# Sample attention scores: the query at 8r of 32 columns, a column strip per chunk, and a new order around it

## The chip, the cores and the metric

One core of one Trainium2 chip runs the whole program. The metric is the device time of one execution in microseconds (us). TensorE is PE in the profile (its weight loads PEld), VectorE DVE, ScalarE ACT, GpSimd POOL, the DMA-issuing SyncE SP.

## The reference, cut to what matters

The program is one decoder layer: an input projection, latent attention and retention, their merge, a convolutional feed-forward. It works on a prompt of 512 + 16 tokens and on 8 samples of one token each, with a paged cache of 4096 positions per sample. The change touches only the latent attention of the samples:

```
q_abs = einsum('bthn,chn->bthc', q_nope, w_uk)                     # 8 heads, 256 latent dims
s_past = einsum('bthc,bsc->bhts', q_abs, c_past) + einsum('bthr,bsr->bhts', q_rope, kr_past)
s_new  = einsum('bthc,buc->bhtu', q_abs, c_new) + einsum('bthr,bur->bhtu', q_rope, kr_new)
p = softmax(concat([s_past, s_new]) * scale)
o_lat = einsum('bhts,bsc->bthc', p_past, c_past) + einsum('bhtu,buc->bthc', p_new, c_new)
```

c_past is 4096 x 256 and kr_past 4096 x 32 for each of the 8 samples. Everything is float32.

## The kernel before

Each engine has its own program; semaphores tie them. Prompt attention comes before the stage of interest, the merge and the feed-forward after it. The stage handles the 8 samples one after the other. A sample's pages are cut into 8 chunks of 512 positions. POOL gathers a chunk (512 KB) with one indirect DMA (`chunk`, line 569) into `pages_c`, which has two halves, one for even and one for odd samples; a gather overwrites what the sample two before had there. In POOL's loop (lines 595 to 604) the gather of chunk c waits until PE has weighed chunk c of that earlier sample (`pv_chunk`, line 1984); the rope rows and the indices of the sample wait for `s_full`, the earlier sample's finished scores.

On PE, one call of `sample` (line 1989) is one step. A step mixes two samples: it scores sample b, and for sample b - 1 does the softmax's small parts and the weighing. Its blocks:
- `turn_chunk` (line 1910): eight 128 x 128 transposes bring a chunk's latent dims onto the partitions, into PSUM banks 0, 1 (even chunks) or 2, 3 (odd). ACT (`even_back`) or DVE (`odd_back`) copies them to `pages_T`; the next turn into the same banks waits for that copy. `pages_T` holds four chunks, so a copy also waits until the chunk four before has been scored.
- `score_pair` (line 1922): two chunks at once. The stationary operand is the query, 32 columns of which 8 (the heads) are filled; the four pages r of a chunk go to the four strips of 32 columns, 256 moving columns each. ACT copies the results (`parts_back`) and `add_parts` turns them with small matmuls onto bank 6, on which `score_rope` has put the rope part (one matmul a chunk, 128 stationary and 32 moving columns).
- `score_new` adds the sample's own token; DVE then takes the scores and their maxima (`scores_back`).
- `max_turn`, `max_spread`, `sum_spread`: the maximum over partitions and the sum, each a small PE operation between two DVE operations; `exp_sample` on ACT lies between them.
- `weigh_chunk` (line 1974): probabilities times pages, four matmuls a chunk in the four strips. The first waits for the exponentials and for the reciprocal of the sum (`inv_sum`).
- `latent_turn`: the weighted sum back onto partitions, after DVE's copy (`outputs_back`).

The order on each engine is written out by hand in `sample` (PE), `sample_dve` (DVE) and `sample_act` (ACT). PE weighs chunks 0 and 1 of sample b - 1 after the second score pair, 2 to 4 after the third, then turns chunks 0 and 1 of sample b + 1 (whose gathers went into the half just weighed), and weighs 5 to 7 after the fourth pair. Steps 1 to 6 gather again in this way; the pages of samples 0 and 1 are gathered ahead of the stage.

Of the kernel before, what the change touches and what calls it, by code (L numbers as in the profile page):

```python
# [146 lines left out]
def build(nc, ins, outs):  # L147
    ctx = ExitStack()
    with ctx:
# [53 lines left out]
        def plan(start, *items):  # L203
# [34 lines left out]
        (PGR, SCB, PB, QRB, SSM, OL, SPART, OPART, QNW, QRW), e4 = plan(  # L238
# [40 lines left out]
        def score_width(t):  # L279
# [20 lines left out]
                 "rope_back chunk_turned odd_turned ct_act ct_dve pair_scored q_staged parts_back "  # L300
# [314 lines left out]
        def _(act):  # L615
# [211 lines left out]
            ct, scored, shifted = Count(S["chunk_turned"]), Count(S["pair_scored"]), Count(S["shifted"])  # L827
            rope_t = Count(S["rope_turned"])

            def even_back(c, reuse=0):  # L830
                act.wait_ge(ct.sem, ct.after())
                if reuse:
                    act.wait_ge(scored.sem, scored.after(reuse))
                nc.scalar.activation(CT[:, c % 4].rearrange("p a b -> p (a b)"),
                                     PS[:, 0:2, :].rearrange("p a b -> p (a b)"), ACT.Copy
                                     ).then_inc(S["ct_act"], 1)
# [5 lines left out]
            def parts_back(a):  # L842
                act.wait_ge(scored.sem, scored.after())
                nc.scalar.activation(SPART[:, a, :], PS[:, 4 + a, :], ACT.Copy).then_inc(S["parts_back"], 1)
# [30 lines left out]
            sample_act(1, True, False)  # L875
            exp_sample(1)
# [122 lines left out]
        def _(dve):  # L999
# [311 lines left out]
            V.memset(PB[:, :, 33:36, :], 0.0).then_inc(S["olat_ready"], 1)  # L1311
# [3 lines left out]
            ct_o, s_full, scored = Count(S["odd_turned"]), Count(S["s_full"]), Count(S["pair_scored"])  # L1315
# [4 lines left out]
            def stage_query(par, b):  # L1320
                V.tensor_copy(QNW[:, par, :, 0:HEADS], QAB[:, :, bass.ds(b, 1), :].rearrange("p a b h -> p a (b h)"))
# [3 lines left out]
            def odd_back(c, reuse=True):  # L1325
                dve.wait_ge(ct_o.sem, ct_o.after())
                if reuse:
                    dve.wait_ge(scored.sem, scored.after())
                V.tensor_copy(CT[:, c % 4].rearrange("p a b -> p (a b)"),  # L1329
# [46 lines left out]
            def sample_dve(par, b, prev=True, more=True, first=False):  # L1376

                if prev:
                    max_rows(1 - par)
                odd_back(3, not first)  # L1380
                if prev:
                    shift(1 - par)
                    sum_rows(1 - par)
                odd_back(5)
                if prev:
                    inv_sum(1 - par)
                if more:
                    stage_query(1 - par, b + 1)
                odd_back(7)
                if more:  # L1390
                    odd_back(1)
                if prev:
                    outputs_back()
                scores_back(par, b)
                if prev:
                    latent_out(1 - par, b - 1)

            stage_query(0, 0)
            odd_back(1, False)
            sample_dve(0, 0, prev=False, first=True)  # L1400
            with loop(dve, 3, {chain: 4, ct_o: 8, scored: 8, mxt: 2, mxs: 2, exp_s: 2, sums: 2, s_full: 2,
                               bank_free: 2, pv_full: 2, lat_turned: 2}) as i:
                for par in range(2):
                    sample_dve(1 - par, i * 2 + (1 + par))
            sample_dve(1, DEC - 1, more=False)
            max_rows(1)
# [165 lines left out]
        def _(pe):  # L1572
# [349 lines left out]
            def score_pair(par, p):  # L1922


                two_chunks = slice(2 * (p % 2), 2 * (p % 2) + 2)
                for ct in range(2):
                    for r in range(4):
                        last = T.matmul(PS[32 * r:32 * r + 32, 4 + p // 2, 256 * (p % 2):256 * (p % 2) + 256  # L1928
                                           ].rearrange("p (a b) -> p a b", a=2),
                                        QNW[:, par, ct, :], CT[:, two_chunks, ct, P * r:P * (r + 1)],  # L1930
                                        start=ct == 0, stop=ct == 1, skip_group_check=True)
                last.then_inc(S["pair_scored"], 1)

            def score_rope(par, c):
# [270 lines left out]
```

## Time and profile before

| | us |
|---|---|
| median of 3 runs (lowest, highest) | 1296.41 (1295.78, 1297.62) |
| profiled execution, its own time | 1295.44 |
| its span, first to last instruction | 1293.6 |
| PE busy | 1151.9 (89%) |
| DVE, ACT, POOL busy | 562.7, 399.2, 109.0 |
| mean granted PE clock | 0.935 |

A clock of 1.00 is 2.4 GHz, 0.50 is 1.2 GHz. In rows in order of time, the first number is the start from the span's begin, the second the duration of the merged instructions, xN their count; an idle time of the engine ahead of them and its releaser stand in brackets. An f32 matmul appears as two instructions, a transpose as one.

### The profile page before, as it was taken

The numbers are of one execution on the slowest core, as the hardware profiler recorded it, in microseconds if no ns is written. First come the engines' busy times: TensorE is split into PE (matmuls) and PEld (weight loads), VectorE is DVE, ScalarE is ACT, GpSimd is POOL, SyncE is SP. The second block draws the span as 40 slices with busy tenths as digits, with TensorE's granted clock in tenths as the row PEclk, the third lists the DMA queues.
The fourth block names the chain that finished last, engine by engine and source line by source line (L and its number), as shares of the span: only waits on it lengthen the run. The fifth ranks groups of instructions, "written<-read, shape, count | busy, mean of one in ns | idle before, by whom it ended". The sixth has DMA issues, their size and how long they took to land.

```text
span 1293.6 us, 22217 instructions
## 1 busy us (share of the span) xinstructions
PE 1151.9 (89%) x9006; PEld 1044.0 (81%) x9006; DVE 562.7 (44%) x901; ACT 399.2 (31%) x645; POOL 109.0 (8%) x99
## 2 busy tenths in 40 slices
PE   2899988879999997999996889679999999999991
PEld 1899887767878786777774889679999999999991
DVE  7256643363534444343342451644444213444226
ACT  3222321213232423323331122344553123443112
POOL 3000002000000002243420000210000000000003
PEclk9989997879999998999996899769999999999995
DMA  9312347113314002475642564113322253232201
GB/s 271 98 52 66 83 99 234 48 33 89 84 31 115 33 33 85 145 243 195 225 166 83 153 174 121 33 34 97 85 77 73 73 146 99 80 83 61 82 21 69
DMA packets 168466, 131.67 MB, mean 102 GB/s; under 512 B 19052, under 2 KB 151489, under 8 KB 168401
## 3 DMA queue, kind: packets, MB, share of 16 engines
q1 hardware_dynamic: 155880, 88.95, 24.8%
q0 software_dynamic: 10368, 37.75, 8.5%
q10 hardware_dynamic: 2176, 4.39, 0.9%
q8 instruction: 29, 0.48, 0.2%
q14 instruction: 13, 0.10, 0.0%
HBM read 119.27 MB, written 11.90 MB: 101 GB/s over the span
## 4 chain that ended last, share of the span: by engine, by line
PE 82%; DVE 11%; ACT 2%; issue 2%; DMA 1%; POOL 0%; SPq 0%; POOLq 0%; ACTq 0%; DVEq 0%; PEldq 0%
PE PS L1584 47%; PE PS L1790 8%; PE PS L1918 5%; PE PS L1595 3%; PE PS L1981 3%; PE PS L1928 2%; PE PS L1828 2%; DVE stats L1028 1%; PE PS L1935 1%; PE PS L1817 1%; DVE y_tok L1033 1%; DVE x_tok L1033 1%; PE PS L1942 1%; PE PS L1805 1%; DVE w_lo L1010 1%
## 5 line engine op out<-in xcount | busy, mean ns | idle before, releaser
L1584 PE MATMUL PS<-x_hi,w_hi 128*128 128x268 f32 x1056 | 226.6, 297 | 8.0 <-DVE w_lo L1010 4.0
L1584 PE MATMUL PS<-x_lo,w_hi 128*128 128x268 f32 x1056 | 222.0, 292 | 0.0
L1584 PE MATMUL PS<-x_hi,w_lo 128*128 128x268 f32 x1056 | 221.1, 292 | 0.0
L1010 DVE TENSOR_TENSOR w_lo<-w_raw,w_hi 128x2048 fp32r<-128x2048 f32 (+3 forms) x65 | 130.6, 2009 | 160.8 <-ACT w_hi L628 160.5
L1584 PEld LDWEIGHTS PS<-x_hi,w_hi 128*128 128x128 f32 x1056 | 171.4, 196 | 12.9 <-DVE w_lo L1010 4.4
L1584 PEld LDWEIGHTS PS<-x_lo,w_hi 128*128 128x128 f32 x1056 | 171.3, 195 | 0.0
L1584 PEld LDWEIGHTS PS<-x_hi,w_lo 128*128 128x128 f32 x1056 | 169.8, 194 | 0.0
L628 ACT ACTIVATE w_hi<-w_raw 128x2048 fp32r<-128x2048 f32 (+3 forms) x65 | 109.5, 1684 | 119.5 <-PE PS L1584 75.1
L1790 PE MATMUL PS<-x_hi,w_hi 128*128 128x268 f32 x256 | 79.7, 311 | 0.0
L1584 PE MATMUL PS<-ffn_hi,w_hi 128*128 128x268 f32 x352 | 73.8, 292 | 5.2 <-DVE ffn_lo L1525 5.2
L1790 PE MATMUL PS<-x_hi,w_lo 128*128 128x268 f32 x256 | 74.3, 290 | 0.0
L1790 PE MATMUL PS<-x_lo,w_hi 128*128 128x268 f32 x256 | 74.2, 290 | 0.0
L549 POOL TENSOR_TENSOR y_tok<-y_tok,ln_gb 128x1024 f32<-128x1024 f32 (+1 forms) x10 | 23.4, 2343 | 596.6 <-ACT y_tok L641 596.6
L1584 PE MATMUL PS<-ffn_hi,w_lo 128*128 128x268 f32 x352 | 73.4, 290 | 0.0
L1584 PE MATMUL PS<-ffn_lo,w_hi 128*128 128x268 f32 x352 | 73.1, 289 | 0.0
L1918 PE MATMUL PS<-square_consts,pages_c 128*128 128x128 f32 x512 | 64.1, 279 | 6.9 <-DVE q_now L1312 6.3
L569 POOL DMA_INDIRECT pages_c<-in_cache_kv_latent_dram,page_rows_now x64 | 61.9, 968 | 82.2 <-PE PS L1981 67.9
L1329 DVE COPY pages_T<-PS 128x1024 f32<-128x1024 f32 x32 | 39.2, 1224 | 66.6 <-PE PS L1918 62.5
L1918 PEld LDWEIGHTS PS<-square_consts,pages_c 128*128 128x128 f32 x512 | 57.2, 144 | 13.4 <-issue 13.1
L1584 PEld LDWEIGHTS PS<-ffn_hi,w_hi 128*128 128x128 f32 x352 | 56.2, 193 | 5.7 <-issue 5.7
L1584 PEld LDWEIGHTS PS<-ffn_lo,w_hi 128*128 128x128 f32 x352 | 56.1, 192 | 0.0
L1584 PEld LDWEIGHTS PS<-ffn_hi,w_lo 128*128 128x128 f32 x352 | 56.0, 192 | 0.0
(291 smaller groups left out, 1847.3 us busy)
## 6 DMA issues: line engine op xcount, KB each, us to landing
w_raw<-in_w_ffn_in_dram SPq DMA_DIRECT2D x44, 512.0 KB, 5.0
w_raw<-in_w_in_dram SPq DMA_DIRECT2D x37, 512.0 KB, 6.2
w_raw<-in_w_ffn_out_dram SPq DMA_DIRECT2D x16, 384.0 KB, 3.9
w_raw<-in_w_ffn_out_dram SPq DMA_DIRECT2D x16, 320.0 KB, 3.5
gate_scratch<-gate_out ACTq DMA_DIRECT2D x8, 536.0 KB, 2.9
gates<-gate_scratch SPq DMA_DIRECT2D x8, 536.0 KB, 4.9
w_raw<-in_w_o_dram SPq DMA_DIRECT2D x8, 512.0 KB, 5.1
x_tok<-in_x_prompt_dram SPq DMA_DIRECT2D x4, 512.0 KB, 8.0
```

Source lines behind the costliest of these rows:

```text
L569: nc.gpsimd.indirect_dma_start(out=PGC[:, par, 4 * c:4 * c + 4, :].rearrange("p r c -> p (r c)"), out_offset=None, in_=lat_rows, in_offset ...
L628: nc.scalar.activation(WH[:, par, 0:nk], RAW[:, par, 0:nk], ACT.Copy).then_inc(s_whi, 1)
L1010: V.tensor_tensor(WL[:, par, 0:nk], RAW[:, par, 0:nk], WH[:, par, 0:nk].bitcast(F32), ALU.subtract).then_inc(s_wsplit, 1)
L1033: V.scalar_tensor_tensor(x[0:r, t, :], x[0:r, t, :], MV[0:r, t, 0:1], gain[0:r, 0, :], ALU.subtract, ALU.mult).then_inc(chain.sem, 1)
L1329: V.tensor_copy(CT[:, c % 4].rearrange("p a b -> p (a b)"), PS[:, 2:4, :].rearrange("p a b -> p (a b)")).then_inc(S["ct_dve"], 1)
L1584: last = T.matmul(PS[:, bank, 0:HALF], w[:, par, k, m * P:(m + 1) * P], x[:, k0 + k, half * HALF:(half + 1) * HALF], start=start and k == ...
L1595: last = T.matmul(PS[:, 2 * p + half, 0:HALF], a, b[:, half * HALF:(half + 1) * HALF], start=i == 0, stop=i == len(lhs) - 1)
L1790: last = T.matmul(PS[:, half, 0:HALF], w[:, par, k, m * P:(m + 1) * P], x[:, k, half * HALF:(half + 1) * HALF], start=k == 0 and w is WH a ...
L1828: last = T.matmul(out, VB[0:w, k, rows_], PTS[0:w, hh, k, 0:r], start=k == 0, stop=k == t)
L1918: last = T.transpose(PS[:, 2 * (c % 2) + ct, P * r:P * (r + 1)], PGC[:, par, 4 * c + r, ct * P:(ct + 1) * P], IDENT)
L1928: last = T.matmul(PS[32 * r:32 * r + 32, 4 + p // 2, 256 * (p % 2):256 * (p % 2) + 256].rearrange("p (a b) -> p a b", a=2), QNW[:, par, ct ...
L1981: last = T.matmul(PS[32 * r:32 * r + 32, 7, 256:256 + KVL], PB[:, par, k:k + 4, :].rearrange("p k h -> p (k h)"), PGC[:, par, k, :], start ...
```

## The change

- The staged query has four copies, copy r with the 8 heads at columns 8r of 32. `score_half` scores four chunks (a = 0 for chunks 0 to 3, a = 1 for 4 to 7) at once: chunk g goes to column strip g, page r accumulates through copy r of the query, so that one strip's 32 rows are 4 pages x 8 heads and a matmul has 128 moving columns. It is called in two halves, pages 0 and 1, then 2 and 3; the second half also adds the rope part, one matmul a chunk, into the same strips.
- The results of four chunks are one 128 x 128 tile; `turn_parts` turns it with one transpose.
- `pages_T` holds eight chunks, so fewer copies wait for scores; `rope_T` moves elsewhere, `score_parts` shrinks to 128 columns.
- The order in `sample`, `sample_dve` and `sample_act` is new: the second half of a sample's second group of scores, its parts, `score_new` and `scores_back` lie in the next step, and `latent_turn` lies in the step after the weighing. Chunks 0 to 3 are weighed in one block just ahead of the turn of the next sample's chunk 0, and 4 to 7 in another. What was left over from step 7 follows it. POOL's program is not changed.

```diff
-        (PGR, SCB, PB, QRB, SSM, OL, SPART, OPART, QNW, QRW), e4 = plan(
+        (PGR, SCB, PB, QRB, SSM, OL, SPART, OPART, QNW, QRW, RTT), e4 = plan(
             65536, ("pages_r", [P, 2, NPAGES, ROPE]), 
...
-            ("score_parts", [P, 2, 512]), ("out_parts", [P, KVL]), ("q_now", [P, 2, 2, 32]), ("q_rope_now", [P, 2, 32]))
-
-        CT = nc.alloc_sbuf_tensor_at("pages_T", [P, 4, 2, 512], F32, offset=base)
-        RTT = nc.alloc_sbuf_tensor_at("rope_T", [P, 2, NCH, P], F32, offset=base + 4 * 2 * 512 * 4)
-        assert (4 * 2 * 512 + 2 * NCH * P) * 4 <= 2 * KT * COLS * 4
+            ("score_parts", [P, 2, P]), ("out_parts", [P, KVL]), ("q_now", [P, 2, 2, 4, 32]), ("q_rope_now", [P, 2, 32]),
+            ("rope_T", [P, 2, NCH, P]))
+
+        CT = nc.alloc_sbuf_tensor_at("pages_T", [P, NCH, 2, 512], F32, offset=base)
+        assert NCH * 2 * 512 * 4 <= 2 * KT * COLS * 4
 
...
 
                 even_back(2)
                 if prev:
+                    parts_back(1)
+                even_back(4)
+                if prev:
                     exp_sample(1 - par)
-                even_back(4, 1)
+                even_back(6)
                 parts_back(0)
-                even_back(6)
                 if more:
+                    even_back(0)
                     rope_back(1 - par, 0, 4)
-                    even_back(0, 1)
-                else:
-                    scored.add()
-                parts_back(1)
-                if more:
                     rope_back(1 - par, 1, 4)
 
...
+                    V.tensor_copy(QNW[:, par, :, r, HEADS * r:HEADS * (r + 1)],
+                                  QAB[:, :, bass.ds(b, 1), :].rearrange("p a b h -> p a (b h)"))
                 V.tensor_copy(QRW[:, par, :], QRB[:, bass.ds(b, 1), :, :].rearrange("p b g h -> p (b g h)")
                               ).then_inc(S["q_staged"], 1)
 
-            def odd_back(c, reuse=True):
+            def odd_back(c, wait=1):
...
                 V.tensor_copy(OPART[:], PS[:, 7, 256:256 + KVL]).then_inc(S["o_parts"], 1)
 
-            def sample_dve(par, b, prev=True, more=True, first=False):
-
+            def sample_dve(par, b, prev=True, more=True, older=True):
+
+                if prev and older:
+                    outputs_back()
+                odd_back(3, 0)
+                if prev:
+                    if older:
+                        latent_out(par, b - 2)
+                    scores_back(1 - par, b - 1)
+                odd_back(5, 2 if prev else 0)
                 if prev:
                     max_rows(1 - par)
-                odd_back(3, not first)
+                    shift(1 - par)
+                odd_back(7, 0)
                 if prev:
-                    shift(1 - par)
                     sum_rows(1 - par)
-                odd_back(5)
-                if prev:
                     inv_sum(1 - par)
                 if more:
                     stage_query(1 - par, b + 1)
-                odd_back(7)
-                if more:
-                    odd_back(1)
-                if prev:
-                    outputs_back()
-                scores_back(par, b)
-                if prev:
...
-                T.matmul(PS[:, 6, 32 * c:32 * c + 32], RTT[:, par, c, :], QRW[:, par, :], start=c == 0, stop=False,
-                         skip_group_check=True)
-
-            def add_parts(a):
+            def score_half(par, a, half):
+
+
+                for r in range(2 * half, 2 * half + 2):
+                    for ct in range(2):
+                        for g in range(4):
+                            last = T.matmul(PS[32 * g:32 * g + 32, 4 + a, 0:P], QNW[:, par, ct, r, :],
+                                            CT[:, 4 * a + g, ct, P * r:P * (r + 1)], start=r == 0 and ct == 0, stop=False,
+                                            skip_group_check=True)
+                if half:
+                    for g in range(4):
+                        last = T.matmul(PS[32 * g:32 * g + 32, 4 + a, 0:P], QRW[:, par, :], RTT[:, par, 4 * a + g, :],
+                                        start=False, stop=True, skip_group_check=True)
+                last.then_inc(S["half_scored"], 1)
+
+            def turn_parts(a):
 
                 pe.wait_ge(parts.sem, parts.after())
-                for c in range(4):
-                    T.matmul(PS[:, 6, 32 * (4 * a + c):32 * (4 * a + c) + 32], SPART[:, a, P * c:P * (c + 1)],
-                             SMALL[:, 26:58], start=False, stop=a == 1 and c == 3, skip_group_check=True)
+                T.transpose(PS[:, 6, P * a:P * (a + 1)], SPART[:, a, :], IDENT)
 
             def score_new(par):
                 out = PS[0:DEC, 6, 256:264]
                 for ct in range(2):
-                    T.matmul(out, CN8[:, ct, :], QNW[:, par, ct, 0:HEADS], start=False, stop=False, skip_group_check=True)
...
                     T.matmul(PS[0:HEADS, 7, 256:256 + KVL], PB[0:DEC, par, 32, :], CTX[0:DEC, :], start=False, stop=True,
                              skip_group_check=True).then_inc(S["pv_full"], 1)
 
-            def sample(par, prev=True, more=True):
+            def sample(par, prev=True, more=True, older=True):
 
 
                 turn_chunk(par, 2)
+                if prev and older:
+                    latent_turn()
                 turn_chunk(par, 3)
                 if prev:
-                    pe.wait_ge(olat.sem, olat.after())
-                    max_turn(1 - par)
+                    score_half(1 - par, 1, 1)
+
+                turn_chunk(par, 4)
+                if prev:
+                    turn_parts(1)
+                    score_new(1 - par)
+                turn_chunk(par, 5)
                 pe.wait_ge(q_staged.sem, q_staged.after())
                 pe.wait_ge(rope_back.sem, rope_back.after(1 if prev else 2))
-                score_pair(par, 0)
+                score_half(par, 0, 0)
+                if prev:
+                    if older:
+                        pe.wait_ge(olat.sem, olat.after())
+                    max_turn(1 - par)
+
+                turn_chunk(par, 6)
                 if prev:
                     max_spread(1 - par)
-
-                turn_chunk(par, 4)
-                turn_chunk(par, 5)
-                score_pair(par, 1)
+                turn_chunk(par, 7)
+                score_half(par, 0, 1)
                 if prev:
                     sum_spread(1 - par)
-                    pe.wait_ge(bank_free.sem, bank_free.after())
-                for c in range(4):
-                    score_rope(par, c)
-                if prev:
-                    for c in range(2):
-                        weigh_chunk(1 - par, c)
-
-                turn_chunk(par, 6)
-                turn_chunk(par, 7)
-                score_pair(par, 2)
-                for c in range(4, 6):
-                    score_rope(par, c)
-                add_parts(0)
-                if more:
-                    turn_rope(1 - par, 0, 4)
-                if prev:
-                    for c in range(2, 5):
+                    for c in range(4):
                         weigh_chunk(1 - par, c)
 
                 if more:
                     turn_chunk(1 - par, 0)
+                    if prev:
+                        pe.wait_ge(bank_free.sem, bank_free.after())
+                    turn_parts(0)
                     turn_chunk(1 - par, 1)
+                    turn_rope(1 - par, 0, 4)
                 else:
+                    pe.wait_ge(bank_free.sem, bank_free.after())
+                    turn_parts(0)
                     pe.wait_ge(ct_a.sem, ct_a.after())
                     pe.wait_ge(ct_d.sem, ct_d.after())
-                score_pair(par, 3)
-                for c in range(6, NCH):
-                    score_rope(par, c)
+                score_half(par, 1, 0)
                 if prev:
-                    for c in range(5, NCH):
+                    for c in range(4, NCH):
                         weigh_chunk(1 - par, c)
                 if more:
                     pe.wait_ge(rope_back.sem, rope_back.after())
                     turn_rope(1 - par, 1, 4)
-                add_parts(1)
-                score_new(par)
-                if prev:
-                    latent_turn()
 
             rope_back, q_staged, parts = Count(S["rope_back"]), Count(S["q_staged"]), Count(S["parts_back"])
...
```

On ACT `parts_back` now waits for two `half_scored` and copies 128 columns; the loops on PE and DVE run twice two steps, with steps 0, 1, 6 and 7 written out.

## Rows read from the trace of the kernel before

**Rows 1.** The page: busy time, share and instructions; the chain by engine.
```profile
PE 1151.9 (89%) x9006; PEld 1044.0 (81%) x9006; DVE 562.7 (44%) x901; ACT 399.2 (31%) x645; POOL 109.0 (8%) x99
...
PE 82%; DVE 11%; ACT 2%; issue 2%; DMA 1%; POOL 0%; SPq 0%; POOLq 0%; ACTq 0%; DVEq 0%; PEldq 0%
```

**Rows 2.** One step; busy time (x instructions) by engine, PE clock, DMA share, GB/s.
```profile
555.45:577.64 22.19, 22.19 (x251) 16.27 (x251) 8.53 (x19) 6.80 (x9) 8.65 (x11) 1.00 0.63 209
```

**Rows 3.** The same step, PE in order of time: start, duration, instruction, count.
```profile
557.43 1.07 PE L1928 MATMUL PS<-pages_T,q_now 128*32 128x256 f32 x16
558.43 0.38 PE L1958 MATMUL PS<-sm,square_consts 8*128 8x8 f32 x2
558.74 1.97 PE L1918 MATMUL PS<-square_consts,pages_c 128*128 128x128 f32 x16
560.64 1.07 PE L1928 MATMUL PS<-pages_T,q_now 128*32 128x256 f32 x16
561.64 0.39 PE L1963 MATMUL PS<-sm,square_consts 128*128 128x8 f32 x2
561.88 1.06 PE L1935 MATMUL PS<-q_rope_now,rope_T 128*128 128x32 f32 x8
562.87 1.07 PE L1981 MATMUL PS<-pages_c,p_sample 128*32 128x256 f32 x16
563.87 1.97 PE L1918 MATMUL PS<-square_consts,pages_c 128*128 128x128 f32 x16
...
567.24 1.06 PE L1942 MATMUL PS<-small_consts,score_parts 128*128 128x32 f32 x8
568.13 0.63 PE L1905 MATMUL PS<-square_consts,pages_r 128*128 128x128 f32 x4
568.70 1.50 PE L1981 MATMUL PS<-pages_c,p_sample 128*32 128x256 f32 x24
570.13 1.97 PE L1918 MATMUL PS<-square_consts,pages_c 128*128 128x128 f32 x16
...
577.64 1.95 PE L1918 MATMUL PS<-square_consts,pages_c 128*128 128x128 f32 x16
```

**Rows 4.** POOL in order of time: the gather of chunk 0.
```profile
564.35 0.94 POOL L569 DMA_INDIRECT pages_c<-in_cache_kv_latent_dram,page_rows_now  x1 [6.07 <-PE PS L1981]
```

**Rows 5.** Gathers' line 569, issue to landing: those issued at 564.35, 565.59, 571.42.
```profile
DMA to landing us min/median/max: 4.3/4.3/4.3
...
DMA to landing us min/median/max: 5.1/5.1/5.1
...
DMA to landing us min/median/max: 5.8/5.8/5.8
```

**Rows 6.** DVE and PE in order of time: one copy, then the tail.
```profile
565.88 1.23 DVE L1329 COPY pages_T<-PS 128x1024 f32<-128x1024 f32 x1 [3.11 <-PE PS L1918]
...
686.83 0.37 PE L1954 MATMUL PS<-square_consts,sm 128*8 128x128 f32 x1 [0.85 <-DVE o_lat L1367]
...
689.37 0.62 DVE L1356 TENSOR_REDUCE sm<-p_sample 128x8 f32<-128x264 f32 x1 [0.49 <-ACT p_sample L840]
...
690.05 0.60 PE L1963 MATMUL PS<-sm,square_consts 128*128 128x8 f32 x2 [1.63 <-DVE sm L1356]
691.04 6.37 PE L1981 MATMUL PS<-pages_c,p_sample 128*32 128x256 f32 x64 [0.39 <-DVE sm L1361]
```

**Rows 7.** Windows as in rows 2 at three places, and PE's first instruction after a pause.
```profile
512.40:515.60 3.20, 3.20 (x17) 3.20 (x16) 0.00 (x0) 1.85 (x3) 2.46 (x3) 0.50 0.94 321
515.80:519.20 3.40, 2.87 (x30) 2.36 (x32) 1.53 (x2) 1.09 (x2) 2.49 (x4) 1.00 0.98 361
...
737.60:744.30 6.70, 6.15 (x27) 6.16 (x28) 5.63 (x7) 1.80 (x2) 0.00 (x0) 0.50 0.02 2
...
738.15 0.81 PE L1584 MATMUL PS<-attn_hi,w_hi 128*128 128x268 f32 x2 [3.63 <-DVE w_lo L1010]
```

More of the change, by code:

```diff
@@ L842, in parts_back @@
             def parts_back(a):
-                act.wait_ge(scored.sem, scored.after())
-                nc.scalar.activation(SPART[:, a, :], PS[:, 4 + a, :], ACT.Copy).then_inc(S["parts_back"], 1)
+                act.wait_ge(scored.sem, scored.after(2))
+                nc.scalar.activation(SPART[:, a, :], PS[:, 4 + a, 0:P], ACT.Copy).then_inc(S["parts_back"], 1)
             def rope_back(par, half, bank):
@@ L1320, in stage_query @@
             def stage_query(par, b):
-                V.tensor_copy(QNW[:, par, :, 0:HEADS], QAB[:, :, bass.ds(b, 1), :].rearrange("p a b h -> p a (b h)"))
+                for r in range(4):
+                    V.tensor_copy(QNW[:, par, :, r, HEADS * r:HEADS * (r + 1)],
+                                  QAB[:, :, bass.ds(b, 1), :].rearrange("p a b h -> p a (b h)"))
                 V.tensor_copy(QRW[:, par, :], QRB[:, bass.ds(b, 1), :, :].rearrange("p b g h -> p (b g h)")
                               ).then_inc(S["q_staged"], 1)
-            def odd_back(c, reuse=True):
+            def odd_back(c, wait=1):
                 dve.wait_ge(ct_o.sem, ct_o.after())
-                if reuse:
-                    dve.wait_ge(scored.sem, scored.after())
-                V.tensor_copy(CT[:, c % 4].rearrange("p a b -> p (a b)"),
+                if wait:
+                    dve.wait_ge(scored.sem, scored.after(wait))
+                V.tensor_copy(CT[:, c].rearrange("p a b -> p (a b)"),
                               PS[:, 2:4, :].rearrange("p a b -> p (a b)")).then_inc(S["ct_dve"], 1)
@@ L1388, in sample_dve @@
                     stage_query(1 - par, b + 1)
-                odd_back(7)
-                if more:
-                    odd_back(1)
-                if prev:
-                    outputs_back()
-                scores_back(par, b)
-                if prev:
-                    latent_out(1 - par, b - 1)
+                    odd_back(1, 2)
             stage_query(0, 0)
-            odd_back(1, False)
-            sample_dve(0, 0, prev=False, first=True)
-            with loop(dve, 3, {chain: 4, ct_o: 8, scored: 8, mxt: 2, mxs: 2, exp_s: 2, sums: 2, s_full: 2,
+            odd_back(1, 0)
+            sample_dve(0, 0, prev=False)
+            sample_dve(1, 1, older=False)
+            with loop(dve, 2, {chain: 4, ct_o: 8, scored: 8, mxt: 2, mxs: 2, exp_s: 2, sums: 2, s_full: 2,
                                bank_free: 2, pv_full: 2, lat_turned: 2}) as i:
                 for par in range(2):
-                    sample_dve(1 - par, i * 2 + (1 + par))
+                    sample_dve(par, i * 2 + (2 + par))
+            sample_dve(0, DEC - 2)
             sample_dve(1, DEC - 1, more=False)
+            outputs_back()
+            latent_out(0, DEC - 2)
+            scores_back(1, DEC - 1)
             max_rows(1)
@@ L1947, in score_new @@
                 for ct in range(2):
-                    T.matmul(out, CN8[:, ct, :], QNW[:, par, ct, 0:HEADS], start=False, stop=False, skip_group_check=True)
+                    T.matmul(out, CN8[:, ct, :], QNW[:, par, ct, 0, 0:HEADS], start=ct == 0, stop=False,
+                             skip_group_check=True)
                 T.matmul(out, KR8[:], QRW[:, par, 0:HEADS], start=False, stop=True, skip_group_check=True
@@ L2053, in _ @@
             sample(0, prev=False)
+            sample(1, older=False)
             per = {ct_a: 8, ct_d: 8, bank_free: 2, mx: 2, dg: 2, sums: 2, rs: 2, olat: 2,
@@ L2056, in _ @@
             per.update({pages[j][c]: 1 for j in range(2) for c in range(NCH)})
-            with loop(pe, 3, per):
+            with loop(pe, 2, per):
                 for par in range(2):
-                    sample(1 - par)
+                    sample(par)
+            sample(0)
             sample(1, more=False)
+            latent_turn()
+            score_half(1, 1, 1)
+            turn_parts(1)
+            score_new(1)
             pe.wait_ge(olat.sem, olat.after())
```

25 lines of the change are left out of this document (7 added, 18 removed).

## The prediction

> **What bounds the kernel now.** I read four views in this order. The page first: PE is busy 89% of the span and 82% of the chain of waits is PE's, so a microsecond matters where PE runs without a gap [rows 1]. Then the busy time of one stage: in the sample scores, steps of 22.19 us (577.64 - 555.45), PE is busy all 22.19 us at granted clock 1.00 (2.4 GHz), DVE 8.5, ACT 6.8, POOL 8.6 [rows 2]. So PE's own instructions set the step; what other engines wait for costs nothing yet. Then PE in order of time, for the price of each block as the distance to the next block's start [rows 3]. Last the loop through PE, POOL and the gathers, which has no idle in it on PE today but little slack either [rows 3 to 5].
>
> **Prices of the blocks** [rows 3]. Two chunk turns (16 transposes) and the change to the scoring form: 560.64 - 558.74 = 1.90 us; a transpose alone is 0.109 (1.90 less 0.16 for the change of form, over 16), a chunk 0.87. A score_pair: 558.43 - 557.43 = 1.00 for 16 halves (every f32 matmul is issued as two). They run as four groups, one half in each 32-column strip at once: 1.00 = 4 x 0.215 + 0.14 for leaving the form. 256 columns in two passes at 2.4 GHz are 0.213, so the stream sets these 0.215. Rope matmuls: 8 halves 562.87 - 561.88 = 0.99. add_parts: 568.13 - 567.24 = 0.89 for 8 halves. Both load 128 columns for 32 that stream: 0.111 each. Weighing: 563.87 - 562.87 = 1.00 for two chunks, 570.13 - 568.70 = 1.43 for three, so 1.86 for four.
>
> **The matmuls.** Per sample the change takes out four pairs (4.00), eight rope matmuls (16 halves, about 2.02 with their changes of form) and eight part matmuls (1.80). It adds 64 score matmuls of 128 columns and 8 rope matmuls in the same strips: 144 halves, 36 groups of four. No row before has 32 stationary columns and 128 moving. Bounds of a group: the stream, half of 0.215 = 0.107; and 0.215, should a group of any width take what today's takes. I take 0.108: a transpose loads 128 columns and streams 128 in 0.109, so load and stream overlap fully there, and four strips of 32 columns load as much [rows 3]. 36 x 0.108 + 4 x 0.14 for the forms = 4.45. Two transposes of the parts add 0.22. Further the weighing goes in two blocks of four instead of 2, 3, 3 chunks: -0.14. Sum: 22.19 - 7.82 + 4.45 + 0.22 - 0.14 = 18.9; laying the after order out block by block gives 18.66, which I use: 3.5 us less PE work a step.
>
> The Trainium skill (TensorE: Matmul & The Clock Gate, section "Wait — 56ns, not 53.3ns?") gives a floor of about 62 ns per matmul where instructions go through the sequencer's code. A group of four would take 0.248 by it, whatever its width. The trace has such a group in 0.215 and single halves of rope at 0.111, so it does not bear the 62 ns out at once; the 0.215 end is rival two below.
>
> **What the new order uncovers.** I lay out step b from the start S of the turn of chunk 2.
> (a) S + 0 turn 2, latent_turn (four halves at 0.111 = 0.45), turn 3, second half of the last sample's second scores (1.22), turn 4, parts, new; turn 5 at S + 4.8; first half scores; maximum; turn 6; spread (0.31, [rows 3]); turn 7 at S + 8.2.
> (b) sum_rows now stands behind the copy of chunk 7 on DVE. Such a copy starts 1.14 after its turn (565.88 against 563.87 + 0.87) and takes 1.23, of which the next instruction overlaps a little: 1.16; PE's sum_spread starts 0.68 after the sum's start (690.05 - 689.37) [rows 3, 6]. So sum_spread is at turn 7 + 2.98, where PE alone would have it at + 2.26: a wait of 0.72.
> (c) Weighing waits for the reciprocal, and the four score_rope (0.99) that lay between are gone. sum_spread's two halves take 0.39, and at the tail, where nothing lies between either, PE idled 0.39 more for the reciprocal [rows 3, 6]: 0.78 where it is 0.24 today (561.88 - 561.64), a wait of 0.54. Weighing starts at W = S + 11.9. PE alone with (b) and (c) would need 19.9 a step.
> (d) The large one. Both samples' pages lie in two buffers. Chunk 0 of the next sample goes where chunk 0 of the last one is just being weighed, and POOL's gather waits for that. Today weighing starts at 562.87, POOL issues at 564.35 (+1.48) and the gather lands 4.3 later, at +5.8; PE wants it at 570.13, +7.3. The second chunk lands at 565.59 + 5.1 = +7.8, wanted at +8.1 [rows 3 to 5]. It is just in time. After the change turn 0 stands directly behind four weighed chunks: it wants chunk 0 at W + 1.86. The gather is unchanged: PE waits to W + 5.9, 4.0 us. Then the parts' transpose and turn 1, ready at W + 6.9, wants a gather that lands at W + 7.9: 1.0 more.
> (e) Rope turn and changes of form (568.70 - 568.13 = 0.57), scores (0.86), then weighing 4 to 7 at V. A burst's second gather takes 5.8 [rows 5]: chunk 5 lands at V + 2.72 + 5.8 = V + 8.5. The next S is at V + 2.9, its turn 5 at V + 7.7: a wait of 0.1 (landing 5.1) to 0.9; I take 0.5. In this part DVE, ACT and POOL (8.6 us of issue a step) are ahead of PE.
> (f) The clock. PE idles some 3.6 us in (d). After 3.63 us idle it was granted 0.50 (1.2 GHz) in 737.60 to 744.30 [rows 7]. At half clock turn 0 (0.87 more) hides in the wait for chunk 1, turn 1 and rope do not. From 0.7 us, if the clock is back after turn 1, to 2.2 us, if it covers rope and scores too; I take 1.1.
> Here the Trainium skill (TensorE: Matmul & The Clock Gate, Part 4: PE-mode transpose) says that transposes don't count as busy for the clock. Then it would stay low through turn 0, turn 1 and rope, and (f) would be 2.2 a step. The trace speaks against it: in 512.40 to 515.60 PE does transposes alone at 0.50, and in 515.80 to 519.20, begun with transposes, the clock is 1.00 [rows 7].
>
> A step: 19.9 + 4.0 + 1.0 + 0.5 + 1.1 = 26.5 against 22.2: +4.3.
>
> **The ends.** Step 0 weighs nothing and its next pages landed long before: it gains the matmul saving, and a half scoring of 1.2 us moves into step 1 instead; against it stand larger memset and staging copies ahead of the first turn (0.3) and a wait of 0.5 for the copy of chunk 3 on DVE. -3.7. Steps 1 to 6 gather again: 6 x 4.3 = 25.8, less 0.9 in step 1, which has no latent_turn and no late chunk 5: +24.9. Step 7 turns no next sample, so no (d); but latent_turn, half the second scores (1.2), parts and new now follow it with nothing beside them, and latent_turn waits 1.2 for its copy. By the blocks 22.7 us from its S to the maximum's transpose, against 686.83 - (577.64 + 4 x 22.19) = 20.4 [rows 3, 6]: +2.3. The rest of the kernel is untouched.
> -3.7 + 24.9 + 2.3 = +23.5. The profiled execution took 1295.44 us (span 1293.6 and 1.8 around it): 1318.9. The median of the runs is 0.97 above it, so **1320 us**.
>
> **Rivals.**
> One, the likeliest: as above, 80%. Without the clock's loss (-6.6) and the late chunk 5 (-3) it is 1310; with no wait for the sum either (-4.3) 1306; with 2.2 for the clock (+6.6) 1326, with chunk 5 at 0.9 and groups at 0.13 (0.8 a step) 1333.
> Two, narrower groups are no cheaper (0.215): 32 groups beyond today's cost add 36 x 0.107 = 3.9 a step, of which 0.7 hides in the wait of (b): 7 x 3.2 = +22, 1342. For it: no row of that form; against: the 0.215 is the stream's own time. 8%.
> Three, faster: the gather is not late. It needs issue to landing of some 1 us instead of 4.3 and 5.1 for chunks 0 and 1, or a POOL that runs ahead. Then the step is 19.9, six of them -13.7, ends -1.9 with (b) and (c) inside: 1281. For it: the gathers move 209 GB/s at DMA share 0.63 only, so DMA has room [rows 2]; against: 4.3 was measured for a gather with nothing ahead of it. It decides from the step's 22.2: waits and clock together under 2.5 of the 6.6 us I count. 6%.
> Four, gains and losses meet: landing waits of about 2.5 a step and no clock loss, 1296. 3%. The remaining 3% is slower by a little, 1300 to 1306, where half of (d) is covered.
>
> **The numbers.** One holds 1306 to 1333. Outside lie rivals two to four and the last case; the range 1306 to 1331 leaves out about 2 in 10. This kernel's runs can tell 0.2% (2.6 us). Faster 0.06, the same 0.03, slower 0.91.
>
> **What would show it.** PE idle ahead of the turn of chunk 0, released by a gather, six times some 3.6 us, the second turn also waiting; POOL's first gather still 1.48 after the first weighed chunk; granted clock under 1.00 in the sample stage, where it was 1.00 throughout; step length 25 to 28 for steps 1 to 6; the mean PE time of the score line, 144 x 8 halves, near 0.027 each without idle; sum_spread released by DVE's sum, and weighing by the reciprocal. I am wrong if PE has no idle before chunk 0, if the groups of four are 0.2 apart, or if the clock stays at 1.00 (then 1313).

## The result and the profile after

| | before | after |
|---|---|---|
| median, us | 1296.1 (4 runs) | 1324.17 (1321.02 to 1325.53, 4 runs) |
| ratio to before | | 1.0218, 95% interval 1.0189 to 1.0246 |
| profiled execution; span | 1295.44; 1293.6 | 1323.69; 1321.8 |
| stage, first turn to the last sample's max_turn | 175.3 (511.58 to 686.83) | 204.5 (510.92 to 715.37) |

The forecast was 1320 (1306 to 1331). The change is slower by 28 us, all of it in the sample stage (+29.2).

The page after, busy time and chain, against [rows 1]: PE is busy for 9.6 us less in a span 28 us longer, and DMA's share of the chain goes from 1% to 6%.

```profile
PE 1142.3 (86%) x9406; PEld 1044.8 (79%) x9406; DVE 564.5 (43%) x925; ACT 393.9 (30%) x645; POOL 108.9 (8%) x99
...
PE 75%; DVE 12%; DMA 6%; issue 3%; ACT 2%; POOL 0%; SPq 0%; POOLq 0%; ACTq 0%; DVEq 0%; PEldq 0%
```

One step after in windows (columns as in [rows 2]): the step itself, 27.86 us instead of 22.19, and the stretch in it at half clock. PE is busy 22.1 of 27.9 us, and part of that at 0.50.

```profile
583.59:611.45 27.86, 22.12 (x301) 17.38 (x300) 8.58 (x21) 6.16 (x9) 8.45 (x11) 0.88 0.51 171
...
601.95:608.65 6.70, 5.91 (x55) 5.06 (x57) 1.23 (x1) 1.62 (x2) 0.00 (x0) 0.50 0.48 172
```

PE in order of time in that step, from the spread of the maximum on (columns as in [rows 3]; the bracket is the idle time ahead and who ended it). Weighing starts at 595.57. The turn of chunk 0 starts at 601.44 after 3.94 us of idle ended by a gather, that of chunk 1 at 604.03 after 0.79 more. In [rows 3] neither turn had a bracket.

```profile
591.53 0.38 PE L1960 MATMUL PS<-sm,square_consts 8*128 8x8 f32 x2
591.85 1.09 PE L1922 MATMUL PS<-square_consts,pages_c 128*128 128x128 f32 x8
592.87 1.08 PE L1932 MATMUL PS<-pages_T,q_now 128*32 128x128 f32 x32
593.77 0.40 PE L1937 MATMUL PS<-rope_T,q_rope_now 128*32 128x128 f32 x8
594.79 0.39 PE L1965 MATMUL PS<-sm,square_consts 128*128 128x8 f32 x2 [0.62 <-DVE sm L1356]
595.57 1.93 PE L1983 MATMUL PS<-pages_c,p_sample 128*32 128x256 f32 x32 [0.39 <-DVE sm L1361]
601.44 1.59 PE L1922 MATMUL PS<-square_consts,pages_c 128*128 128x128 f32 x8 [3.94 <-DMA pages_c<-in_cache_kv_latent_dram,page_rows_now]
602.82 0.42 PE L1944 MATMUL PS<-square_consts,score_parts 128*128 128x128 f32 x1
604.03 1.97 PE L1922 MATMUL PS<-square_consts,pages_c 128*128 128x128 f32 x8 [0.79 <-DMA pages_c<-in_cache_kv_latent_dram,page_rows_now]
605.80 1.06 PE L1909 MATMUL PS<-square_consts,pages_r 128*128 128x128 f32 x4
606.79 1.94 PE L1932 MATMUL PS<-pages_T,q_now 128*32 128x128 f32 x32
608.50 2.01 PE L1983 MATMUL PS<-pages_c,p_sample 128*32 128x256 f32 x32
```

POOL's first two gathers in that step, which answer to [rows 4]: 597.04 is 1.47 behind the start of weighing, as 1.48 before. They landed 4.3 and 5.7 us later.

```profile
597.04 0.94 POOL L569 DMA_INDIRECT pages_c<-in_cache_kv_latent_dram,page_rows_now  x1 [6.39 <-PE PS L1983]
598.28 0.94 POOL L569 DMA_INDIRECT pages_c<-in_cache_kv_latent_dram,page_rows_now  x1 [0.30 <-issue]
```

Steps 2 and 4, each whole and then its stretch at half clock (columns again as in [rows 2]). Steps 1 and 4, with such a stretch of some 3.4 us, took 25.7 and 25.9; step 2, with 6.8 us of it, 28.7.

```profile
554.92:583.59 28.67, 22.14 (x302) 17.07 (x300) 8.67 (x21) 6.15 (x9) 8.83 (x11) 0.88 0.52 167
574.65:581.35 6.70, 5.73 (x56) 4.56 (x60) 1.22 (x1) 1.53 (x2) 0.00 (x0) 0.50 0.42 149
...
611.46:637.32 25.86, 20.54 (x302) 16.50 (x301) 8.67 (x21) 6.15 (x9) 8.65 (x11) 0.93 0.57 182
629.25:632.55 3.30, 2.81 (x13) 2.82 (x14) 0.00 (x0) 0.81 (x1) 0.56 (x1) 0.50 0.98 338
```

### The profile page after: what moved, and what is told of

The parts are those of the page before. It is cut to its first block, busy times and chain, and to the rows that moved or that the text cites. A ratio compares the mean times of both kernels' runs of the same rounds, so it can differ in the third digit from the quotient of the medians.

```text
span 1321.8 us, 22989 instructions
## 1 busy us (share of the span) xinstructions
PE 1142.3 (86%) x9406; PEld 1044.8 (79%) x9406; DVE 564.5 (43%) x925; ACT 393.9 (30%) x645; POOL 108.9 (8%) x99
## 4 chain that ended last, share of the span: by engine, by line
PE 75%; DVE 12%; DMA 6%; issue 3%; ACT 2%; POOL 0%; SPq 0%; POOLq 0%; ACTq 0%; DVEq 0%; PEldq 0%
PE PS L1588 45%; PE PS L1794 8%; DMA pages_c<-in_cache_kv_latent_dram,page_rows_now 4%; PE PS L1922 4%; PE PS L1599 3%; PE PS L1832 2%; PE PS L1983 2%; PE PS L1932 2%; DVE stats L1025 1%; PE PS L1821 1%; DVE y_tok L1030 1%; DVE x_tok L1030 1%; DVE w_lo L1007 1%; PE PS L1809 1%; DMA w_raw<-in_w_attn_out_dram 1%
## 5 line engine op out<-in xcount | busy, mean ns | idle before, releaser
L1922 PE MATMUL PS<-square_consts,pages_c 128*128 128x128 f32 x512 | 77.0, 301 | 37.0 <-DMA pages_c<-in_cache_kv_latent_dram,page_rows_now 29.4
L1922 PEld LDWEIGHTS PS<-square_consts,pages_c 128*128 128x128 f32 x512 | 64.0, 156 | 44.7 <-issue 28.1
```

The costliest lines, as they stand in the source:

```text
L1922: last = T.transpose(PS[:, 2 * (c % 2) + ct, P * r:P * (r + 1)], PGC[:, par, 4 * c + r, ct * P:(ct + 1) * P], IDENT)
```

## The experiments

Theory A is the forecast's: the gather stands directly ahead of its user, and the idle time halves the clock. B: the new score code or DVE's order is the loss. C and D came up on the way. Times on different chips differ (the kernel before took 1295 to 1302 in these comparisons), so ratios and steps are what to compare. Where "steps" have one length, it is the average of steps 1 to 6.

**E1, the changed kernel without the later gathers.** PE's wait for pages becomes a constant that is already reached:

```diff
-                        pool.wait_ge(weighed.sem, weighed.after())
-                        pool.sem_inc(S["go_on"])
-                        chunk(par, c)
```

> The changed kernel without the 48 chunk gathers of samples 2 to 7: the pages of samples 0 and 1 are scored and weighed again, so PE, DVE and ACT do the same work and nothing waits for a gather (rope rows are still gathered). Theory A (the late gather and the clock it costs): no PE idle ahead of chunk 0, granted clock 1.00 in the stage, steps 1 to 6 of 19.9 us instead of 27.2, execution 1324 - 6 x 7.3 = 1280 us, 15 under the kernel before. Rival B (the packed score matmuls or DVE's new order are the loss): steps stay above 24 us, execution above 1305 us. Mixed: each us of step over 19.9 is B's.

Measured: 1281.02, ratio 0.9865 (0.9827 to 0.9902). The step is 20.2 us at clock 1.00, PE busy 19.1 of it:

```profile
574.73:594.95 20.22, 19.09 (x301) 15.12 (x300) 8.66 (x21) 6.16 (x9) 1.15 (x2) 1.00 0.10 28
```

So the matmul saving is real, and B falls: everything over 20.2 us a step, 7.0 us of the 27.2, needs the gathers. PE in order of time gives the price of the end of a step at full clock, from the turn of chunk 1 to the next step: 594.95 - 589.80 = 5.15 us.

```profile
589.80 1.04 PE L1918 MATMUL PS<-square_consts,pages_c 128*128 128x128 f32 x8
...
594.95 1.04 PE L1918 MATMUL PS<-square_consts,pages_c 128*128 128x128 f32 x8
```

**E2, the kernel before, the same left out.**

> The kernel before with the same 48 gathers left out, as the control of the run above. Theory A: in the old order every gather lands before PE wants it, so the step stays 22.2 us and the time 1296 us (within 0.3%). If gathers slow the old kernel too (shared memory traffic, small waits), the step falls below 22.0 and the gain of the run above is partly of that kind.

Measured: 1295.49 (one run), step 22.20 as with gathers. The old order pays nothing for them.

```profile
582.83:605.03 22.20, 22.20 (x251) 16.28 (x250) 8.58 (x17) 6.81 (x9) 1.15 (x2) 1.00 0.08 24
```

**E4, the kernel before with its weighing moved down alone.**

```diff
-                if prev:
-                    for c in range(2):
-                        weigh_chunk(1 - par, c)
...
-                    for c in range(2, 5):
+                    for c in range(5):
```

> The kernel before, its score code and its ACT and DVE order untouched, with the weighing of chunks 0 and 1 moved down to stand with 2 to 4, directly ahead of the turn of the next sample's chunk 0. Theory A: weighing of chunk 0 to landing of its gather stays 5.8 us, PE wants it 2.3 after, so it waits 3.5, then about 1.1 for chunk 1, and loses 1 to 2.5 to the half clock: steps 1 to 6 of 27.5 to 29 us instead of 22.2, execution 1328 to 1337 us. Rival B (the new score code is the loss): about 1296 us.

Measured: 1358.03 (one run), worse than either theory had it (A: 1328 to 1337). PE in order of time: weighing at 583.20, the turn of chunk 0 5.96 later. The wait is as forecast (3.60 and 0.97); the clock is not.

```profile
583.20 2.37 PE L1981 MATMUL PS<-pages_c,p_sample 128*32 128x256 f32 x40
589.16 1.09 PE L1918 MATMUL PS<-square_consts,pages_c 128*128 128x128 f32 x8 [3.60 <-DMA pages_c<-in_cache_kv_latent_dram,page_rows_now]
591.22 1.97 PE L1918 MATMUL PS<-square_consts,pages_c 128*128 128x128 f32 x8 [0.97 <-DMA pages_c<-in_cache_kv_latent_dram,page_rows_now]
```

In windows, 16.9 us at half clock followed that one wait, with PE busy 16.2 of them:

```profile
590.50:607.40 16.90, 16.18 (x97) 11.36 (x101) 3.08 (x7) 3.03 (x4) 4.07 (x6) 0.50 0.62 207
```

Four of the steps had that, two had 6.8 us; they averaged 32.1 us. Weighing directly ahead of the turn, with the old score code, makes the whole loss and more. That the clock stayed low for so much longer here than in the changed kernel is not explained.

**E3, the wait filled with small transposes** (36 ahead of chunk 0, 8 ahead of chunk 1):

```diff
+                for _ in range(fill):
+                    T.transpose(PS[:, 2 * (c % 2), 0:P], IDENT, IDENT)
                 pe.wait_ge(pages[par][c].sem, pages[par][c].after())
```

> The changed kernel with PE's wait for the gathers filled: 36 transposes of a constant (0.109 us each, 3.9 us) ahead of the wait for chunk 0 and 8 (0.87 us) ahead of chunk 1, in steps 1 to 6, into a bank that the turn then overwrites. Theory A with the clock as its second part: the wait stays as long but the clock stays 1.00, steps become 19.9 + 4.0 + 1.0 + about 0.3 = 25.3 us instead of 27.2, the execution 1324 - 6 x 1.9 = 1312 us, although PE does 29 us more work. Rival (the clock costs nothing, the excess over the forecast is elsewhere): 1324 or more.

Measured: 1322.86, ratio 1.0196 (1.0153 to 1.0239): a miss. The clock did stay at 1.00 in the stage, yet steps were 26.9. PE stood still some 0.6 to 0.9 us, with further slow stretches around it, in the score matmuls of each next step, released by "issue", that is by nothing the profile shows. From the turn of chunk 1 to the next step it took 5.21 us (615.03 - 609.82), E1's 5.15: the clock's loss was gone there, and the standstill took its place.

**E7, the same with few large matmuls**, to see whether the number of instructions does that:

```diff
-                    T.transpose(PS[:, 2 * (c % 2), 0:P], IDENT, IDENT)
+                    T.matmul(PS[:, 2 * (c % 2), :], IDENT, SQ[:, 0:4, :].rearrange("p a b -> p (a b)"), start=True, stop=True)
```

> The changed kernel with PE's waits for the gathers filled as in the earlier filled run, but by 4 matmuls of 512 columns (0.87 us each, 8 instruction pairs) and 1 ahead of chunk 1, instead of 44 transposes. In the earlier run the clock stayed at 1.00 but PE then stood still 1.3 us in each step, released by nothing the profile shows (issue), in the score groups that follow. Theory A (that standstill is the supply of instructions, which the many small ones used up): no such gaps, clock 1.00, steps of 25.4 us against 27.2, execution 1324 - 11 = 1313 us. Rival (the clock's share is nothing, any filled wait brings the same): steps 26.9 as before and 1322.

Measured: 1324.92, ratio 1.0164 (1.0126 to 1.0203), steps 27.1: a second miss, at the rival's 1322 and 26.9 and not at A's 1313. In PE's order of time the standstill is still there, in the same place, so the number of fillers was not it:

```profile
590.02 1.07 PE L1934 MATMUL PS<-pages_T,q_now 128*32 128x128 f32 x25
592.14 0.35 PE L1934 MATMUL PS<-pages_T,q_now 128*32 128x128 f32 x4 [1.06 <-issue]
```

From the start of this half to the next turn it is 2.73 us (592.75 - 590.02) where the same block takes 1.23 after (587.06 - 585.83). Without those 1.5 us the step would be 25.6: that is theory A's 25.4, but worked out, not run. That the clock has a price all the same is seen without this run: the changed kernel took 7.42 us from the turn of chunk 1 to the next step (611.45 - 604.03) in the step shown, where E1 takes 5.15.

**E5, the gap filled by the step's own work.** All eight chunks are weighed in one block, then come parts, rope and scores, and the next chunks 0 and 1 last:

```diff
                     sum_spread(1 - par)
-                    for c in range(4):
+                    for c in range(NCH):
                         weigh_chunk(1 - par, c)
+                    pe.wait_ge(bank_free.sem, bank_free.after())
+                turn_parts(0)
+                if more:
+                    turn_rope(1 - par, 0, 4)
+                pe.wait_ge(ct_a.sem, ct_a.after())
+                pe.wait_ge(ct_d.sem, ct_d.after())
+                score_half(par, 1, 0)
+                if more:
+                    pe.wait_ge(rope_back.sem, rope_back.after())
+                    turn_rope(1 - par, 1, 4)
+                    turn_chunk(1 - par, 0, False)
+                    turn_chunk(1 - par, 1, False)
...
```

> The changed kernel with PE's order changed once more: after sum_spread all eight chunks are weighed in one block, then the parts' transpose, the rope turn, the first half of the second scores, the second rope turn, and only then the turns of the next sample's chunks 0 and 1; ACT copies the rope tiles ahead of chunk 0. No work added or left out. Theory A: the work between the start of weighing and the turn of chunk 0 is 3.6 + 0.5 + 0.1 + 0.5 + 1.0 + 0.5 = 6.2 us, more than the 5.9 of the gather, so chunk 0's wait is gone, chunk 1 (lands at 7.9, wanted at 7.1) keeps 0.8, and the clock stays 1.00: steps of 12.0 + 7.9 + 0.9 = 20.8 us, execution 1324 - 6 x 6.4 = 1286 us, 10 under the kernel before. Rival (gathers in one burst of eight land later than in fours, as the transfers queue): chunks 4 and 5 come late, steps of 22 us and more, no gain over the kernel before.

Measured: 1345.57, ratio 1.0335 (1.0297 to 1.0372), steps 30.5: a miss by 60 us. The waits for gathers are gone, as theory A has it, and another loss, larger than theirs, has come: 32 score instructions of 1.0 us took 8.9 (PE in order of time):

```profile
610.59 0.51 PE L1932 MATMUL PS<-pages_T,q_now 128*32 128x128 f32 x9
611.54 0.42 PE L1932 MATMUL PS<-pages_T,q_now 128*32 128x128 f32 x4 [0.44 <-issue]
613.02 0.42 PE L1932 MATMUL PS<-pages_T,q_now 128*32 128x128 f32 x4 [1.06 <-issue]
...
615.89 0.62 PE L1932 MATMUL PS<-pages_T,q_now 128*32 128x128 f32 x4 [1.03 <-issue]
617.32 1.11 PE L1932 MATMUL PS<-pages_T,q_now 128*32 128x128 f32 x5 [0.81 <-issue]
618.79 0.61 PE L1932 MATMUL PS<-pages_T,q_now 128*32 128x128 f32 x2 [0.35 <-issue]
619.46 0.90 PE L1909 MATMUL PS<-square_consts,pages_r 128*128 128x128 f32 x3
```

The standstill also brings half clock with it: the clock falls to 0.50 within it and stays there for some 7 us, step after step. And POOL is held as well: ahead of its eighth gather it idles 1.0 to 1.8 us in every step, where the others have 0.30, released by "issue" or "remote", that is by nothing of this core that the profile shows (POOL in order of time):

```profile
614.72 0.94 POOL L569 DMA_INDIRECT pages_c<-in_cache_kv_latent_dram,page_rows_now  x1 [0.30 <-issue]
616.81 0.94 POOL L569 DMA_INDIRECT pages_c<-in_cache_kv_latent_dram,page_rows_now  x1 [1.16 <-remote]
```

**E6, and DVE's sum ahead of the copy of chunk 7** (`sum_rows` moved above `odd_back(7, 0)`).

> As the run before, and on DVE the sum of the probabilities stands ahead of the copy of chunk 7 instead of behind it. Theory A (part b of the forecast): PE's wait of 0.6 to 0.7 us ahead of sum_spread goes, the wait for the reciprocal (0.39) grows a little since the copy now stands ahead of it; steps 0.5 us shorter than in the run before, the execution 3 to 4 us shorter, about 1283 us. Rival: DVE now waits for ACT's exponentials with chunk 7's copy behind it, and the first half of the second scores or the reciprocal comes later by as much: no difference.

Measured: 1344.8, ratio 1.0315 (1.0282 to 1.0347), not told apart from E5. In its trace sum_spread has no idle ahead of it, so the wait of part (b) is gone; what that is worth can't be read beside a standstill of 8 us. The step of 20.8 and the 3 to 4 us that were expected are not shown.

**E8, E5 without the later gathers.** Theory C: PE's instructions come late while gathers are in flight. D: the order itself.

> The reordered kernel (all eight chunks weighed in one block) without the 48 chunk gathers of samples 2 to 7. With the gathers its score matmuls of the first half of the second group took 9 us instead of 0.9 in every step, PE standing still in pieces of 0.3 to 1.1 us that nothing in the profile releases, exactly while POOL's burst of eight gathers was under way. Theory C (PE's instructions come late while gathers are in flight): without them no such gap, steps of 20.0 to 20.3 us as in the changed kernel without gathers, execution about 1281 us. Rival D (the order itself starves PE, through its denser run of small instructions, or waits of ACT and DVE): the gaps stay, steps over 25 us.

Measured: 1287.75 (one run), steps 21.3. The standstill is gone, so D falls; but the steps are 1.1 us over E1's 20.2 and over C's 20.0 to 20.3, so the order has a small cost of its own. PE waits 0.24 us for ACT's copy and 0.32 for DVE's (596.44, 597.85). The block of E5's lines above, in PE's order of time:

```profile
592.25 0.60 PE L1905 MATMUL PS<-square_consts,pages_r 128*128 128x128 f32 x4
592.78 1.08 PE L1928 MATMUL PS<-pages_T,q_now 128*32 128x128 f32 x32
593.80 0.66 PE L1905 MATMUL PS<-square_consts,pages_r 128*128 128x128 f32 x4
```

**E9 to E12, E6 with paced gathers.** POOL waits for the landing of an earlier gather, 2, 3 or 4 chunks back:

```diff
                         pool.wait_ge(weighed.sem, weighed.after())
                         pool.sem_inc(S["go_on"])
+                        if c >= lag:
+                            before = landed[par][c - lag]
+                            pool.wait_ge(before.sem, before.after())
+                            pool.sem_inc(S["go_on"])
                         chunk(par, c)
```

> The reordered kernel with the earlier sum, its gathers paced: POOL issues chunk c only when chunk c - 2 of the same sample has landed, so that at most two are in flight. Theory C: PE's standstill in the score matmuls shrinks from 8 us a step to under 1; each pair of gathers takes about 5 us, eight take 20, so late chunks (4 to 7) come 1 to 3 us late; steps of 21 to 24 us, execution 1283 to 1302 us. Rival D (the order, not the traffic): standstill of 8 us as before and 1345 us or more.

Measured: 1331.24, ratio 1.0245 (1.0211 to 1.0279), steps 27.8 where C had 21 to 24. No standstill, but gathers late by far, and the clock falls again in most steps.

> The same with chunk c - 3, at most three in flight. Theory C: gathers finish sooner (about 1.7 us each, eight in 14), no late chunk, but more standstill than with two: 1 to 4 us a step; steps of 21 to 25 us, execution 1285 to 1310 us. Rival D: as with no pacing, 1345 us.

Measured: 1302.18, ratio 0.9997 (0.9968 to 1.0027), steps 23.1; 0.2 us of standstill a step, clock 1.00.

> The reordered kernel with the earlier sum and its gathers paced at four in flight (chunk c waits for the landing of c - 4). With three in flight PE stood still 0.2 us a step in the score matmuls and waited some 2 us a step for gathers, steps of 23.0 us; with the unpaced burst it stood still 8 us. Theory C (standstill grows with the gathers in flight) and the gather chain shorter by some 4 us: standstill 1 to 2 us a step, gather waits under 1; steps of 21.5 to 23.5 us, execution 1286 to 1302 us. Against C: a standstill of 0.2 or less with four, or of 8 as with the burst.

Measured: 1288.14, ratio 0.9951 (0.9933 to 0.9969), steps 21.9: under the kernel before by 0.5%, which is little but clear of the interval. The clock fell in one of the steps, for some 3.4 us. No standstill at all, which C as written did not have (it wanted more than with three). PE from weighing on:

```profile
584.47 3.66 PE L1992 MATMUL PS<-pages_c,p_sample 128*32 128x256 f32 x64 [0.43 <-DVE sm L1369]
588.06 0.59 PE L1997 MATMUL PS<-c_tok,p_sample 8*8 8x256 f32 x2
588.58 0.33 PE L1953 MATMUL PS<-square_consts,score_parts 128*128 128x128 f32 x1
588.75 0.60 PE L1918 MATMUL PS<-square_consts,pages_r 128*128 128x128 f32 x4
589.28 1.08 PE L1941 MATMUL PS<-pages_T,q_now 128*32 128x128 f32 x32
590.29 0.66 PE L1918 MATMUL PS<-square_consts,pages_r 128*128 128x128 f32 x4
590.78 1.04 PE L1931 MATMUL PS<-square_consts,pages_c 128*128 128x128 f32 x8
592.75 1.09 PE L1931 MATMUL PS<-square_consts,pages_c 128*128 128x128 f32 x8 [0.93 <-DMA pages_c<-in_cache_kv_latent_dram,page_rows_now]
```

> As the run with three in flight for chunks 3 and 4 (their gathers run beside the densest score matmuls), chunk 5 unpaced behind chunk 4, chunks 6 and 7 waiting for the landing of chunks 2 and 3, so up to four or five in flight late. Theory C: standstill in the first half scores stays at 0.2, some 0.5 may come in the second half; the last chunks land 2 to 3 us sooner, so the waits for chunks 4 to 7 (about 1 us a step) go: steps of 21.5 to 22.3 us, execution 1287 to 1293 us, under the kernel before.

Measured: 1292.54, ratio 0.9973 (0.9955 to 0.9991), steps 22.9, over the 21.5 to 22.3 that were expected. No standstill, but waits for gathers in half the turns.

What stays open is what PE stands still for. E6 and E11 differ in POOL's pacing alone, yet E6's score block starts 4.8 us after weighing begins and PE idles in it from 5.3 us on (610.40 and 610.92 against 605.59), while pacing first holds back a gather by more than 0.1 us after 7.8 us: until then POOL had issued the same in both. And E5 and E6 ran on another chip than E8 to E12, while E3 and E7 stood still on two chips. Shown is that the standstill is there with the gathers and was not seen without them (E8) or with four or two in flight. That pacing removes it is argued, and so is that it is late instructions: in two of E5's standstills (640.0 to 650.6 and 672.0 to 681.0) the profile has no packet of a queue that carries instructions. Nor is DMA load alone enough: in [rows 7] PE works 2.87 of 3.40 us beside gathers at 361 GB/s and DMA share 0.98.

## Why the prediction was right

- **(a), the matmuls.** Groups of four at 128 columns: two halves of a score block, 32 instructions, take 593.77 - 592.87 = 0.90 for eight groups, 0.112 each against my 0.108 and the bounds 0.107 and 0.215. Rival two is out, and so are 62 ns for each matmul: four take 0.112 together. The Trainium skill (TensorE: Matmul & The Clock Gate, section "Wait — 56ns, not 53.3ns?") gives the 62 ns for matmuls with hardware decoding off, so this case only shows that they don't bind here. PE's own work came out larger than laid out: 19.1 us busy in E1's step of 20.2, against 18.66 and 19.9.
- **(b), (c).** 0.62 and 0.39 us idle ahead of sum_spread and of weighing, in each of steps 1 to 7; weighing began 11.98 behind the step's start (583.59 to 595.57), forecast 11.9.
- **(d).** In the step shown chunk 0 turned at weighing + 5.87 (forecast 5.9) after 3.94 us idle; in the six steps these idle times were 3.87 to 4.20. Chunk 1 followed at + 8.46, idle 0.79 (forecast 1.0); in steps 4 and 5 it did not wait, as the half clock had made the turn before it longer. E4 shows the same 5.96 with the old code; E1 shows what its absence is worth. Rival three needed a landing 1 us after issue; it was 4.3 again.
- **(e).** Chunk 5 waited 0.18 to 0.65 us in steps 2 and 4 to 7, and not in step 3 (forecast 0.5).
- **(f), the term that was too small.** I took 1.1 us a step. The steps averaged 27.24 against 26.35 (26.5, less the 0.9 of step 1 over six). That is 5.4 of the 5.7 us by which the stage exceeds the forecast. Three of the six steps had 6.8 us at half clock, not 3.4, and were 28.4 us long, the other three 26.1. From the turn of chunk 1 to the next step the first three took 7.97, 7.42 and 8.12 us and the others 6.10, 5.60 and 6.13, where E1 takes 5.15: the clock cost 2.7 and 0.8 us, on average 1.7, and the three longer steps lie above my 0.7 to 2.2. E7 gives 27.2 - 25.6 = 1.6. The rest is PE's own work and the waits of (b) and (c), 20.2 for 19.9, against a chunk 5 that was late by less. What makes the stretch 3.4 or 6.8 us is not explained.
- **Transposes and the clock.** In step 4 PE did transposes alone from 629.74 to 633.56; it was granted 0.50 until 632.55 and, still in the turn of chunk 1, 1.00 from 632.65 on:

```profile
632.65:633.00 0.35, 0.35 (x5) 0.35 (x4) 0.00 (x0) 0.12 (x1) 0.00 (x0) 1.00 0.77 316
```

  That agrees with [rows 7] and speaks against the rule of the Trainium skill (TensorE: Matmul & The Clock Gate, Part 4: PE-mode transpose) that transposes don't count as busy.
- **The ends.** Step 0 took 18.3 against 21.6 (-3.3, forecast -3.7); step 7 took 22.72 to its max_turn (forecast 22.7).

Two terms of opposite sign lie in this change: about -2 us a step of matmul work net of the new DVE waits (E1 against E2: 20.2 against 22.2), and +7 of gather wait and its clock. The forecast had -2.3 and +6.6, so its mechanism holds, and its 1320 is 4 us low because both terms missed in the same direction. The packed matmuls in the old order were not run.

## What to carry to other kernels

When PE sets the time, an order is also a schedule of the buffers' reuse: count from the instruction that frees a buffer, through the issuing engine and the transfer, to its next user (here 5.9 us), and compare that with the work that lies between, not with the engines' mean load. Packing matmuls can pay and still lose if the room it makes was another transfer's cover. After moving such a user away from its gather, look for PE's idle time released by nothing, and try how many gathers should be in flight: here, with the packed matmuls and E6's order, two gave 1.0245 of the time before, three 0.9997 and four 0.9951.

## What the runs showed of the hardware

- An idle stretch of 3.4 to 4.2 us was followed by very different times at half clock: 3.4 or 6.8 us in the changed kernel (idle 3.87 to 4.20), 6.8 or 17 us in E4 (idle 3.37 to 3.79), with PE busy 96% of a stretch of 16.9 us at 0.50.
- PE can stand still for 8 us in the midst of small matmuls, released by nothing that the profile shows, while gathers run; the same matmuls took 1.0 us without gathers (E8) or with them paced (E11). E5 in a window over the gathers, and in the score block alone, where they move 345 GB/s at DMA share 0.97 (columns as in [rows 2]):

```profile
606.00:620.00 14.00, 9.39 (x106) 4.95 (x99) 0.30 (x4) 0.60 (x1) 7.52 (x8) 0.86 0.76 265
...
610.60:619.40 8.80, 4.25 (x33) 1.57 (x32) 0.00 (x0) 0.59 (x1) 4.78 (x6) 0.80 0.97 345
```
